# A three-layer network on one core: tanh for sigmoid in the recurrent and third layers, their vector steps cut or joined, and copies of q, k and u moved to ScalarE

## The reference, cut to what matters

```python
# layer 2, the recurrent unit
y = gelu(y_branch);  xc = causal_depthwise_conv(x_branch, conv_w, conv_b)      # 4 taps
r, i = sigmoid(gates(xc))                        # 8 blocks of 256 x 256
log_a = -8 * r * softplus(-lambda);  a = exp(log_a)
u = sqrt(-expm1(2 * log_a)) * (i * xc)
h[t] = a[t] * h[t - 1] + u[t];       out = (h * y) @ w_out
# layer 3, the S5 half
h[t] = a_bar * h[t - 1] + b_bar @ u[t]           # complex, 4096 states
y = gelu(Re(C h) + D * u);           out = y * sigmoid(y @ w_glu + b_glu)
# layer 3, the attention half: rotary q and k, 8 heads of 128, each with three
# dilations whose softmaxes are mixed by their denominators
```

## Time and profile before

| | us |
|---|---|
| median of 3 runs | 3256.33 (3255.39 to 3256.55) |
| the profiled execution: its own time | 3255.42 |
| its span, first to last instruction | 3253.6 |
| PE busy | 3176.9 (98%), 15119 matmuls |
| DVE busy | 1900.3 (58%) |
| ACT busy | 1570.9 (48%) |
| POOL busy | 246.5 (8%) |

### The profile page before, as it was taken

How to read it: one execution, slowest core, us unless ns; L and a number is a source line. 1 busy time by engine, 2 the same in 40 slices (tenths; PEclk the granted TensorE clock), 3 DMA queues, 4 the chain that set the end, 5 groups by cost and what they waited for, 6 DMA issues and landing times.

```text
span 3253.6 us, 39421 instructions
## 1 busy us (share of the span) xinstructions
PE 3176.9 (98%) x15119; PEld 2621.1 (81%) x15119; DVE 1900.3 (58%) x2186; ACT 1570.9 (48%) x2109; POOL 246.5 (8%) x328
## 2 busy tenths in 40 slices
PE   8999999999999999999999999999989999999998
PEld 6777788888888887778888888888778888888886
DVE  4666754555555767665554555577876545445455
ACT  5655543434444668454444435553354443444444
POOL 0000000000000020010820005620000000000000
PEclk9999999999999999999999999999999999999999
DMA  7444556566666555655656667766535666665664
GB/s 228 143 149 143 182 186 195 188 188 188 192 187 203 175 170 166 191 173 186 194 184 192 188 193 227 246 208 196 163 130 162 195 193 189 190 192 192 190 192 136
DMA packets 324214, 600.70 MB, mean 185 GB/s; under 512 B 33040, under 2 KB 40128, under 8 KB 323776
## 3 DMA queue, kind: packets, MB, share of 16 engines
q1 hardware_dynamic: 321152, 592.94, 58.5%
q10 hardware_dynamic: 2880, 5.24, 0.5%
HBM read 587.09 MB, written 11.01 MB: 184 GB/s over the span
## 4 chain that ended last, share of the span: by engine, by line
PE 89%; DVE 6%; ACT 3%; issue 1%; DMA 0%; SPq 0%; ACTq 0%; DVEq 0%
PE pair L1938 28%; PE pair L1940 28%; PE pair L1939 28%; DVE lo L1182 2%; PE turn_ps L1969 1%; ACT hi L611 1%; PE pair L2284 1%; PE pair L2178 1%; PE pair L2285 0%; DVE conv_o L1285 0%; PE misc_ps L2193 0%; DVE lru_h L1555 0%; DVE xt_l L1444 0%; PE misc_ps L2207 0%; DVE t L1768 0%
## 5 line engine op out<-in xcount | busy, mean ns | idle before, releaser
L1182 DVE TENSOR_TENSOR lo<-raw,hi 128x1024 fp32r<-128x1024 f32 x1084 | 1344.7, 1243 | 1222.0 <-ACT hi L611 1209.0
L611 ACT ACTIVATE hi<-raw 128x1024 fp32r<-128x1024 f32 x1084 | 1144.5, 1060 | 1419.2 <-PE pair L1940 1393.3
L1938 PE MATMUL pair<-hi,xt_h 128*128 128x512 f32 (+1 forms) x2784 | 1100.1, 395 | 26.0 <-DVE lo L1182 11.9
L1940 PE MATMUL pair<-lo,xt_h 128*128 128x512 f32 (+1 forms) x2784 | 1084.9, 390 | 0.0
L1939 PE MATMUL pair<-hi,xt_l 128*128 128x512 f32 (+1 forms) x2784 | 1083.9, 389 | 0.0
L1938 PEld LDWEIGHTS pair<-hi,xt_h 128*128 128x128 f32 x2784 | 524.8, 189 | 148.1 <-issue 18.1
L1940 PEld LDWEIGHTS pair<-lo,xt_h 128*128 128x128 f32 x2784 | 524.7, 188 | 110.1
L1939 PEld LDWEIGHTS pair<-hi,xt_l 128*128 128x128 f32 x2784 | 525.1, 189 | 103.0
L1938 PE MATMUL pair<-hi,ht_h 128*128 128x512 f32 x1504 | 588.4, 391 | 4.9 <-DVE ht_l L1294 3.6
L1940 PE MATMUL pair<-lo,ht_h 128*128 128x512 f32 x1504 | 586.0, 390 | 0.0
L1939 PE MATMUL pair<-hi,ht_l 128*128 128x512 f32 x1504 | 585.9, 390 | 0.0
(11 more groups left out here) (300 smaller groups left out, 1576.5 us busy)
## 6 DMA issues: line engine op xcount, KB each, us to landing
raw<-in_mlp_w SPq DMA_DIRECT2D x512, 512.0 KB, 4.0
raw<-in_w_gate SPq DMA_DIRECT2D x88, 512.0 KB, 4.2
raw<-in_w_up SPq DMA_DIRECT2D x88, 512.0 KB, 4.3
raw<-in_w_down SPq DMA_DIRECT2D x88, 512.0 KB, 4.1
raw<-in_even_w_in SPq DMA_DIRECT2D x68, 512.0 KB, 3.7
raw<-in_odd_w_in SPq DMA_DIRECT2D x64, 512.0 KB, 3.9
raw<-in_w_in SPq DMA_DIRECT2D x64, 512.0 KB, 3.9
raw<-in_even_w_out SPq DMA_DIRECT2D x32, 512.0 KB, 3.7
```

The costliest lines, as they stand in the source:

```text
L611: nc.scalar.activation(hi[:, r], raw[:, slot], ACT.Copy).then_inc(sems["hi_ready"], 1)
L1182: nc.vector.tensor_tensor(lo[:, r], raw[:, slot], hi[:, r].bitcast(F32), ALU.subtract).then_inc(sems["lo_ready"], 1)
L1938: nc.tensor.matmul(to, xh[:, t0 + k, tok], h[:, k], start=s, stop=False)
L1940: mm = nc.tensor.matmul(to, xh[:, t0 + k, tok], l[:, k], start=False, stop=e)
```

## The change

- Sigmoid becomes tanh, with the factor 1/2 taken into scales and later instructions: in the gelu of the recurrent unit, in the S5's gelu and in its gate. One vector instruction (add, then multiply) then takes the place of two in each gelu. The gates of the recurrent unit keep their sigmoid.
- `lru_ratio`: the minimum that guards the square root goes; a constant `guard` is the root's bias instead.
- The turn after a conv chunk comes ahead of unit 2 (3 before). Its taps are made one set a unit, at units 2, 3, 4, in place of all at 3; `split_conv` stays at 5. The last gelu chunk's turn, in the first output chunk, comes ahead of unit 3 (4 before) and its split at 5 (6 before).
- `lru_scan` is parted: the product stays at unit 7 (`lru_drive`), the scans come two by two at units 1 and 2 of the next chunk.
- q, k, u: scalar copies them out of `turn_ps` (`plain`, `halves`). The rotary turn takes both token tiles in one instruction.
- S5: `h_re`, `t_1`, `t_2`, `g_re` lie side by side, so that two rotations are one instruction each way; the eight scans of a group become two over 512 elements, with a stream of `decays`, zero at the start of each state, which scalar writes for each group (a new wait on `b_zeroed` and `scanned` on scalar, on `decayed` on vector). GpSimd clears it once, at slot 8.
- GLU and items: tiles 2 and 3 of y come first (`Y_ORDER`), `y_hi` at slot 61 and the first `y_lo` at 62, each a slot earlier; the last q chunk is turned after the second unit of the GLU, not the third; an item's scores, bias, exp, probabilities and scale come a slot earlier (probabilities in the slot of the exp), its turn and all behind it stay.
- The parameter columns are copied by four instructions in place of two at the start.

The diff, cut to its core (eight leading blanks taken off):

```diff
-t_1, t_2, g_re, g_im = (at(n, 152 + 2 * j, [4, HALF]) for j, n in enumerate(("t_1", "t_2", "g_re", "g_im")))
+s5_v = at("s5_v", 152, [4, 4 * HALF])
+h_re, t_1, t_2, g_re = (s5_v[:, j].rearrange("p (j n) -> p j n", j=4) for j in range(4))
+g_im, h_im = at("g_im", 187.5, [4, HALF])[:], at("h_im", 189.5, [4, HALF])[:]
+decays = at("decays", 200, [4, HALF])
 b_w, c_w = at("b_w", 177, [4, 4, P]), at("c_w", 185, [5, P])
-states = [at("h_re", 187.5, [4, HALF]), at("h_im", 189.5, [4, HALF])]
+states = [h_re, h_im]
...
+Y_ORDER = (1, 0, 2, 3)
...
-    def turn_slot(self, prev, units):
-        return (4 if prev.kind in ("gelu", "rope") else min(3, units - 2)) if prev else -1
+    def turn_slot(self, prev, units, kind):
+        if prev is None:
+            return -1
+        if prev.to[0] == "conv":
+            return 2
+        return 4 if prev.kind == "rope" or prev.kind == "gelu" == kind else min(3, units - 2)
...
-        for a, n in ((0, P + 112), (2 * P, 96)):
-            ins = nc.scalar.activation(col[:, a:a + n], misc_ps[:, 0, a:a + n], ACT.Copy)
+        for a, n, f in ((0, C_BGLU, 1.0), (C_BGLU, 8, 0.5), (C_DSKIP, 8, 1.0), (2 * P, 96, 1.0)):
+            ins = nc.scalar.activation(col[:, a:a + n], misc_ps[:, 0, a:a + n], ACT.Copy, scale=f)
...
-        nc.scalar.activation(tmp[:], tmp[:], ACT.Sigmoid).then_inc(sems["gelu_a"], 1)
+        nc.scalar.activation(tmp[:], tmp[:], ACT.Tanh, scale=GELU_3 / 2).then_inc(sems["gelu_a"], 1)
...
+        elif to[0] == "lru":
             pass
+        elif to[0] in ("plain", "halves"):
+            self.eng.wait_ge(sems["turned"], T.at("turned"))
+            if to[0] == "plain":
+                a = nc.scalar.activation(to[1], turn_ps[:], ACT.Copy)
+            else:
+                a = nc.scalar.activation(to[1].rearrange("p k (two n) -> p k two n", two=2),
+                                         turn_ps[:].rearrange("p k (n two) -> p k two n", two=2), ACT.Copy)
+            a.then_inc(sems["split_done"], 1)
...
-                if j == at + 2 and prev and prev.to[0] in ("conv", "lru"):
+                if prev and (prev.to[0], j) in (("conv", at + 3), ("lru", at + 2)):
                     self.split_conv(prev.to)
...
-        nc.scalar.activation(lru_s[:], lru_s[:], ACT.Sqrt, scale=-1.0).then_inc(sems["lru_root"], 1)
+        nc.scalar.activation(lru_s[:], lru_s[:], ACT.Sqrt, scale=-1.0, bias=guard).then_inc(sems["lru_root"], 1)
...
+        g = s5_step(slot, -1)
+        if g is not None:
+            self.eng.wait_ge(sems["b_zeroed"], 1)
+            if g:
+                self.eng.wait_ge(sems["scanned"], g)
+            nc.scalar.activation(decays[:, :, 1:HALF],
+                                 decay2[:, 4 * g:4 * g + 4].unsqueeze(2).to_broadcast([P, 4, HALF - 1]), ACT.Copy
+                                 ).then_inc(sems["decayed"], 1)
...
-        if slot == 62:
+            self.gelu_tanh(1)
+        if slot == 61:
             self.eng.wait_ge(sems["h_ready"], 8)
             self.y_hi(0)
             self.y_hi(1)
...
-        k = item_step(slot, GLU + 1)
+        k = item_step(slot, GLU)
         if k is not None:
             self.item_exp(k)
-        k = item_step(slot, GLU + 2)
+        k = item_step(slot, GLU + 1)
         if k is not None:
...
-                ins = nc.vector.tensor_scalar(tmp[:], tmp[:], GELU_3, GELU_1, ALU.mult, ALU.add)
-                ins.then_inc(sems["dve_step"], 1)
-                self.eng.wait_ge(sems["dve_step"], T.add("dve_step"))
-                nc.vector.tensor_tensor(tmp[:], tmp[:], stg[:], ALU.mult).then_inc(sems["gelu_b"], 1)
+                nc.vector.scalar_tensor_tensor(tmp[:], tmp[:], GELU_1 / GELU_3, stg[:], ALU.add, ALU.mult
+                                               ).then_inc(sems["gelu_b"], 1)
...
-            for m in range(M):
-                c = small[:, t + 16 * m:t + 16 * m + 16].unsqueeze(1).to_broadcast([P, 4, 16])
-                ins = nc.vector.tensor_tensor(q[:, a, m], xx[:, m], c, ALU.mult)
+            c = small[:, t:t + 32].rearrange("p (m d) -> p m d", m=M).unsqueeze(2).to_broadcast([P, M, 4, 16])
+            ins = nc.vector.tensor_tensor(q[:, a], xx, c, ALU.mult)
         ins.then_inc(sems["dve_step"], 1)
         self.eng.wait_ge(sems["dve_step"], self.T.add("dve_step"))
-        for m in range(M):
-            nc.vector.tensor_tensor(x1[:, m], q[:, 0, m], q[:, 1, m], ALU.subtract)
-            ins = nc.vector.tensor_tensor(x2[:, m], q[:, 2, m], q[:, 3, m], ALU.add)
+        nc.vector.tensor_tensor(x1, q[:, 0], q[:, 1], ALU.subtract)
+        ins = nc.vector.tensor_tensor(x2, q[:, 2], q[:, 3], ALU.add)
...
-            return self.causal_conv(to[1])
+            return self.conv_tap(to[1], 0)
...
+    def conv_tap(self, t0, j):
 
         T = self.T
...
+        if j:
+            self.eng.wait_ge(sems["dve_step"], T.n["tap_at"])
+        else:
+            self.eng.wait_ge(sems["conv_begun"], T.add("conv_begun"))
+        s = 3 - j
+        for k in range(4):
+            c = C_CONV_W + 16 * j + t0 + k
+            a = nc.vector.scalar_tensor_tensor(conv_o[:, k, s:SEQ], turn_ps[:, k, 0:SEQ - s],
+                                               col[:, c:c + 1], conv_o[:, k, s:SEQ], ALU.mult, ALU.add)
+        if j < 2:
+            a.then_inc(sems["dve_step"], 1)
+            T.n["tap_at"] = T.add("dve_step")
+            return
         a.then_inc(sems["conv_done"], 1)
         T.add("conv_done")
...
+                if prev and prev.to[0] == "conv" and j in (at + 1, at + 2):
+                    self.conv_tap(prev.to[1], j - at)
+                if prev and (prev.to[0], j) in (("conv", at + 3), ("lru", at + 2)):
+                    self.split_conv(prev.to)
+                if prev and prev.to[0] == "lru" and j in (1, 2):
+                    self.lru_scan(prev.to[1] // 4, j - 1)
...
-                    self.lru_scan(lru)
+                    self.lru_drive(lru)
...
-        nc.vector.scalar_tensor_tensor(s, s, 1.0, t, ALU.add, ALU.mult).then_inc(sems["dve_step"], 1)
-        self.eng.wait_ge(sems["dve_step"], self.T.add("dve_step"))
-        nc.vector.tensor_scalar(s, s, -2.0 ** -116, None, ALU.min).then_inc(sems["lru_ratio"], 1)
+        nc.vector.scalar_tensor_tensor(s, s, 1.0, t, ALU.add, ALU.mult).then_inc(sems["lru_ratio"], 1)
         self.T.add("lru_ratio")
 
-    def lru_scan(self, q):
+    def lru_drive(self, q):
 
         T, tiles = self.T, slice(4 * q, 4 * q + 4)
         self.eng.wait_ge(sems["gated"], T.add("gated"))
         self.eng.wait_ge(sems["lru_root"], T.add("lru_root"))
-        nc.vector.tensor_tensor(lru_s[:], lru_s[:], lru_x[:, tiles], ALU.mult).then_inc(sems["dve_step"], 1)
-        self.eng.wait_ge(sems["dve_step"], T.add("dve_step"))
-        for k in range(4):
+        nc.vector.tensor_tensor(lru_s[:], lru_s[:], lru_x[:, tiles], ALU.mult).then_inc(sems["lru_driven"], 1)
+
+    def lru_scan(self, q, half):
+
+        self.eng.wait_ge(sems["lru_driven"], q + 1)
+        for k in (2 * half, 2 * half + 1):
             a = nc.vector.tensor_tensor_scan(lru_h[:, 4 * q + k], lru_a[:, k], lru_s[:, k], 0.0, ALU.mult,
                                              ALU.add)
-        a.then_inc(sems["lru_scanned"], 1)
+        if half:
+            a.then_inc(sems["lru_scanned"], 1)
...
+        if slot == 62:
+            self.y_lo(0)
         if slot == 63:
             self.skip(7)
-            self.y_lo(0)
             self.y_lo(1)
...
-        k = item_step(slot, GLU)
+        k = item_step(slot, GLU - 1)
         if k is not None:
             self.item_bias(k)
-        k = item_step(slot, GLU + 1)
+        k = item_step(slot, GLU)
         if k is not None:
             self.item_probs(k)
         k = item_step(slot, GLU + 5)
...
-        nc.vector.tensor_tensor(t_1[:], xr, c, ALU.mult)
-        nc.vector.tensor_tensor(t_2[:], xi, s, ALU.mult)
-        nc.vector.tensor_tensor(g_im[:], xi, c, ALU.mult)
-        nc.vector.tensor_tensor(g_re[:], xr, s, ALU.mult).then_inc(sems["bu_used"], 1)
+        both = rots[g % 2][:].rearrange("p a j n -> p a (j n)")
+        nc.vector.tensor_tensor(s5_v[:, 1:3], pair[1][:], both, ALU.mult)
+        nc.vector.tensor_tensor(g_im, xi, c, ALU.mult)
+        nc.vector.tensor_tensor(g_re, xr, s, ALU.mult).then_inc(sems["bu_used"], 1)
...
     def scan(self, g):
         self.eng.wait_ge(sems["bu_summed"], g + 1)
+        self.eng.wait_ge(sems["decayed"], g + 1)
         for src, dst in ((t_1, t_2), (g_im, g_re)):
-            for j in range(4):
-                t = 4 * g + j
-                a = nc.vector.tensor_tensor_scan(dst[:, j], decay2[:, t:t + 1].to_broadcast([P, HALF]),
-                                                 src[:, j], 0.0, ALU.mult, ALU.add)
+            src, dst, by = (ap.rearrange("p j n -> p (j n)") for ap in (src, dst, decays[:]))
+            a = nc.vector.tensor_tensor_scan(dst, by, src, 0.0, ALU.mult, ALU.add)
         a.then_inc(sems["scanned"], 1)
...
```

(15 more changed lines are left out.)

## The result

The changed kernel takes 3225.78 us (median of four, 3224.76 to 3229.0), the kernel before 3256.44: ratio 0.9908, interval 0.9891 to 0.9925. Forecast was 3230, with 3221 to 3243 as the range. A second set gave 3227.19 beside 3256.40, ratio 0.9909 (0.9893 to 0.9924). The profiled execution is the slowest of the first four, 3229.0 with a span of 3225.7; before it was 3255.4 with 3253.6. So the change saves 26.4 by the own times of the profiled executions, 27.9 by their spans and 29 to 31 by the medians, where my sum had 26.3.

What follows compares the result with a forecast made beforehand. TensorE's pauses, with vector as what it would wait for, were taken as the bound. Savings of 15.9 + 2.6 + 0.6 + 7.6 - 0.4 = 26.3 us from the profiled 3255.4, plus 0.9 to the median, gave 3230; range 3221 to 3243.

Steps and rivals of the forecast that it cites:

- convolution: Recurrent stage, conv chunks: with taps spread over three units, the pauses behind `lo` go, 2.7 us off.
- first gelu chunk: Recurrent stage: with less ahead of the late `lo`, its pause goes but for 0.1, and the clock's fall: 5.7 us.
- three next chunks: Gelu chunks after the first: waits behind `lo` go with the scans, two table-load pauses go with tanh: 3.5 us.
- output chunk: First output chunk: earlier turn and split take 2.7 off the `ht_l` pause, and the clock's fall goes: 4.0 us.
- states, their pauses: State-space groups: joined scans and rotations, shorter rotary and scalar's copies shorten the pauses for states, 2.6 us off.
- the clock's fall there: Among the state groups, near 2313: the pause shrinks but stays, so 0.6 us of at most 1.7 is gained.
- GLU and items: Mixing: pauses for `yt_l`, before the first item's turn and for probabilities shrink or go, table loads too: 7.6 us.
- start: Kernel start: two more parameter copies on scalar ahead of the first `hi` cost at most 0.4 us.
- (a): Scalar's new copies and decays stand in front of `hi` conversions; 11.4 us come back: 3241, chance 0.22.
- (b): Tanh does not join the exponentials' table; loads stay in all chunks and before the first item: 3234, chance 0.06.
- (d): Items: vector's waits use up its lead, each of eight items brings a pause near 3 us: 3267, chance 0.04.
- (c): More goes: clock falls in the GLU and at 2313, and the pause at the item's turn: 3224, chance 0.11.

Runs made afterwards that it cites:

- e5: Changed kernel with the recurrent layer's four scans in one block at the end of a gelu chunk again: 3234.63 us, ratio 0.9934.
- e2: Changed kernel with the recurrent layer's four gelus by sigmoid instead of tanh: 3233.28 us, ratio 0.9926.
- e4: Changed kernel with one gelu by sigmoid, scalar's q copy before the GLU a unit earlier, second half's z split a slot earlier: 3222.61 us, ratio 0.9899.
- e6: Changed kernel with a group's two scans of 512 as eight of 128 again, without scalar's `decays` writes: 3228.88 us, ratio 0.9913.
- e9: e4 plus TensorE's read-out of a group's states one unit later, last group as now: 3214.75 us, ratio 0.9871.
- e10: Kernel before with only the read-out of a group's states a unit later, last group as before: 3244.44 us, ratio 0.9964.
- e3: Changed kernel with the items' steps a slot later and the turn after the third GLU unit, as before: 3226.76 us, ratio 0.9914.
- e7: Changed kernel with the six copies of q, k and u on vector again: 3229.91 us, ratio 0.9923.

## Why the prediction was right, and where not

The mechanism was right: the pauses that were to go went, nearly all by what was named. The sum's closeness is in part luck. The spans differ by 27.9, not 26.3; that the own times differ by 26.4 comes from what they have beyond the span, 1.8 before and 3.3 in the changed kernel. And within the 27.9 the recurrent stage gave 15.5 (forecast 15.9) and the mixing 13.5 (10.8), while 0.3 were lost ahead of the two and 0.8 between them. Term by term, start to start in the two traces:

| term | forecast | found | |
|---|---|---|---|
| convolution | 2.7 | 2.1 | one of four pauses stays, 0.96 |
| first gelu chunk | 5.7 | 4.9 | 0.9 stays |
| three next chunks | 3.5 | 3.2 | 0.1 in the first, 1.6 in each of two |
| output chunk | 4.0 | 4.4 | 1.05 stays for `ht_l`, as forecast |
| states, their pauses | 2.6 | 2.7 | 9.0 in seven to 6.3 in five |
| the clock's fall there | 0.6 | 0.5 | one fall in each trace, to 0.63 and to 0.60 |
| GLU and items | 7.6 | 10.3 | pauses 11.8 to 5.2, both falls of the clock gone |
| start | -0.4 | -0.3 | |

**Convolution.** In the third chunk one pause stays. The delay is as forecast, "under 2 us": against the same matmuls, the `lo` at 1150.63 starts 1.7 later than in the kernel before. What failed is "inside a lead of 8", and the price of a `lo`, "(1.2)". Scalar's, GpSimd's and vector's timelines there:

```profile
1142.56 1.28 ACT L934 ACT_TABLE_LOAD   x1
...
1146.24 1.95 ACT L692 ACTIVATE conv_o<-turn_ps,col 128x256 f32<-128x256 f32 x4
1148.04 1.61 ACT L934 ACTIVATE gate_i<-misc_ps,col 128x256 f32<-128x256 f32 x4
...
1149.83 2.41 POOL L2423 TENSOR_TENSOR lru_h<-ht_h,ht_l 128x1024 f32<-128x1024 f32 x1 [1149.38 <-ACT gate_i L934]
1152.31 3.26 POOL L2534 TENSOR_TENSOR lru_x<-gate_i,lru_h 128x1024 f32<-128x1024 f32 x1
...
1150.63 2.68 DVE L1213 TENSOR_TENSOR lo<-raw,hi 128x1024 fp32r<-128x1024 f32 x1 [0.76 <-ACT hi L624]
...
1154.80 1.85 DVE L1213 TENSOR_TENSOR lo<-raw,hi 128x1024 fp32r<-128x1024 f32 x1
```

I had counted the tap (1.95 it is) and not the gates' table load of 1.28 ahead of it, nor that beside GpSimd's two instructions two `lo` take 2.68 and 1.85 in place of 1.22. The second of them ends the pause, at 1156.7. In the two conv chunks after this one a pair of `lo` takes the same (2.58 and 1.86) and no pause comes; there the gates load no table. So it takes both here, by comparison of chunks; no run removes one of them alone.

**First gelu chunk.** I took everything ahead of `lo` as gone but 0.1. Vector's timeline shows what is left:

```profile
1222.38 1.22 DVE L1587 TENSOR_TENSOR lru_s<-lru_s,lru_x 128x1024 f32<-128x1024 f32 x1
1223.52 1.22 DVE L1232 SCALAR_TENSOR_TENSOR tmp<-tmp,stg 128x1024 f32<-128x1024 f32 x1
1224.65 3.49 DVE L1213 TENSOR_TENSOR lo<-raw,hi 128x1024 fp32r<-128x1024 f32 x3
```

The drive and the gelu's instruction of 1.22 still stand ahead, and then three `lo` in a row without a gap. Start to start the pause went from 4.2 to 0.9, so 3.3 came off: near the 3.1 that I had called certain, while I took the pause as all but gone. The fall of the clock went with it (e5 brings both back, 2.4 of the pause and a clock of 0.63).

**Three next chunks.** The total is near and its shares are wrong. The step "the 0.3 + 0.16 behind `lo` goes with the scans" failed: e5 has the scans back and those waits are not. By elimination they went with the gelu's instruction or the minimum; no run here takes one of these alone. And in the first of the three nothing was gained, since a load was added:

```profile
1225.73 1.28 ACT L666 ACT_TABLE_LOAD   x1
1227.03 1.06 ACT L666 ACTIVATE tmp<-tmp 128x1024 f32<-128x1024 f32 x1
...
1230.14 1.28 ACT L934 ACT_TABLE_LOAD   x1
1231.43 1.57 ACT L934 ACTIVATE gate_r<-pair,col 128x256 f32<-128x256 f32 x4
...
1237.32 1.28 ACT L950 ACT_TABLE_LOAD   x1
```

The tanh of the gelu loads a table, the gates' sigmoids another, the exponentials the first again: four loads with the square root's, where sigmoid, exp, sqrt needed three. The bound was stated (0 to 1.28) and I took zero. The Trainium skill, page ScalarE activation tables: per-element evaluation and per-set limits, section Table sets in the compiler and the runtime, has loads placed per block by greedy longest run, from which I read that tanh would share a table with the sigmoids that follow; the trace disagrees, the load at 1230.14 is there, unless a block ends between the two, which no run here shows. e2 and e4 show the price: 0.3 of a pause, the rest hidden.

**States.** Forecast 2.6, found 2.7, by e6 some 1.3 of it the scans. The working held: 2.25 for the two, rotary's 128-element instructions near 0.28. What I did not see is that the pauses were not a matter of the chain's length. Vector's timeline in the same group has the gaps on the other side:

```profile
2252.96 1.22 DVE L1794 TENSOR_TENSOR s_v<-pair,rot 128x1024 f32<-128x1024 f32 x1 [3.08 <-PE pair L2322]
...
2258.22 1.23 DVE L1213 TENSOR_TENSOR lo<-raw,hi 128x1024 fp32r<-128x1024 f32 x1 [2.84 <-ACT hi L624]
```

Vector waits 3.1 for TensorE's drive and 2.8 for `hi`, and is late by 2.3 at the read-out 13 us later. It had room in the group, but not in its second half. One unit more before the read-out uses that room, e9 and e10.

**GLU and items.** The pause before the turn was forecast at 3.2 with scalar's copy last; it is 2.74 and ends so. That the wait for `xt_l` would grow to 1.5 and one for `xres` come, I missed: I moved the items' steps in my sum and did not ask which work of the GLU's second half then stands behind them; e3 shows it at 0.6 without the move. The credit for "a slot of the item's own chain" was an error as well: e3 gives it back at no cost. The copy carried 1.5 by e7; that the loads and the new order of y carried the rest is by elimination, no run has them alone. The pauses together went from 11.8 to 5.2, near what was forecast. The mis-sized step is the clock, "I let stand but for 0.3": the kernel before has a second fall behind the next pause, for the probabilities,

```profile
2398.90:2403.00 4.10, 4.04 (x21) 4.04 (x22) 4.10 (x8) 2.26 (x5) 0.00 (x0) 0.58 0.41 135
```

and in the changed kernel's profiled execution both are gone, 3.7 us in all. In its second trace one of them is there, below.

**Median and profile.** I added 0.9 to come from profile to median; it should have been taken off, 3. The profiled execution of the changed kernel is the slowest of its set in both sets (span 3225.7, in eight executions 3222.3 to 3225.7), that of before (3253.6) lies near its median: which execution was profiled makes the difference. That fewer pauses leave fewer places for the clock to fall, and so add to the medians, fits the clocks on record but is not shown.

**Rivals.** (a), (b) and (d) did not come true: of `decays` and the copies no trace shows a cost (e6, e7), the exponentials' loads went, and no item stalls TensorE by 3 us. (c) did in part: the clock's falls in the GLU went in the profiled execution, while the one among the states and 2.7 of the turn's pause stayed. The median of 3225.8 is nearer to its 3224 than to the forecast's 3230.

## What to carry to other kernels

Where a busy engine waits for a slow chain on another, look first at that other engine's gaps within the same group of work: if it idles early and is late at the end, moving the consumer one unit later in its own queue can be worth more than shortening the chain (9.0 us of pauses against 2.7 here). Count shorter instructions by what stands ahead of the late one; price each by undoing it alone, as gains of the right total can hide shares that are wrong. When an activation function is exchanged to share a table, check its neighbours on both sides, and use both forms where the neighbours differ.

## What the runs showed of the hardware

A pause of one length brings the granted clock down in some executions and not in others. Stretches of 4 us after the same three pauses (2.51 before group 5's read-out, 1.85 before the next one's, 2.74 before the item's turn), first in the changed kernel's first trace, then in its second, then in e3; the clock is the eighth number:

```profile
2271.50:2275.50 4.00, 3.88 (x42) 3.38 (x43) 3.47 (x4) 1.28 (x2) 0.00 (x0) 0.60 0.98 336
...
2297.50:2301.50 4.00, 4.00 (x58) 3.68 (x59) 3.25 (x3) 0.00 (x0) 0.00 (x0) 1.00 0.97 334
2363.00:2367.00 4.00, 4.00 (x36) 4.00 (x35) 3.93 (x6) 2.34 (x4) 0.00 (x0) 1.00 0.51 145
```

```profile
2268.50:2272.50 4.00, 3.63 (x40) 2.93 (x41) 3.72 (x4) 1.53 (x2) 0.00 (x0) 0.57 0.91 315
2294.80:2298.80 4.00, 4.00 (x48) 3.68 (x47) 3.10 (x3) 0.00 (x0) 0.00 (x0) 0.66 0.96 344
2361.00:2365.00 4.00, 3.43 (x19) 3.46 (x20) 3.97 (x6) 2.28 (x4) 0.00 (x0) 0.58 0.39 130
```

```profile
2271.50:2275.50 4.00, 3.90 (x56) 3.58 (x57) 3.45 (x4) 1.27 (x2) 0.00 (x0) 1.00 0.95 347
2296.50:2300.50 4.00, 4.00 (x60) 3.80 (x50) 2.64 (x3) 0.00 (x0) 0.00 (x0) 1.00 0.99 352
2361.00:2365.00 4.00, 3.94 (x30) 3.84 (x31) 2.84 (x4) 0.95 (x2) 0.00 (x0) 1.00 0.53 163
```

After the first pause the clock fell in two of the three, after the second and the third in one each. Both levels occur after the same work, so a single trace can't tell whether an edit removed a fall; a fall is worth 1.3 to 1.6 us, by the way from each pause to the next in the three traces. What decides it is open.

A scan of 512 elements with a full second operand takes 1.2, on the line of the shorter ones (0.40 for 128, 0.67 for 256). Scalar's `decays` write of 508 elements takes 0.61.

Beside GpSimd's two instructions on `lru_h` and `lru_x` vector's `lo` slows down: all five in the kernel before take 2.58 to 3.42 in place of 1.22, all seven in the changed one 1.86 to 3.36, and a scan of 256 takes 2.82 for 0.67. The taps in the same stretches, which read `turn_ps`, stay at 0.47. Beside GpSimd's other work many `lo` keep their 1.23 and some take up to 2.08, so what counts is not only that GpSimd is busy.
